# A second ring for compression and modulation weights, and their work spread over the attention groups, in a two-layer hybrid trunk

## What is computed

```python
for l in range(DEPTH):
    mod = c_act @ w_mod[l] + b_mod[l]
    shift, scale, gate = jnp.split(mod, 3, axis=-1)
    h = x * (1.0 + scale[:, None, :]) + shift[:, None, :]
    p = h @ w_in[l]
    ...
    # NSA: 2 key/value groups of 3 query heads; three branches per head
    kc = _rope(compress(k_cmp, pe_k, w1_k, w2_k), positions[:, cmp_end])
    vc = compress(v_cmp, pe_v, w1_v, w2_v)
    ...
    # gated delta rule, 6 heads; stick-breaking attention, 4 heads
    y = jnp.concatenate([y_nsa, y_gdn, y_sb], axis=-1) @ w_out[l]
    x = _layernorm(DEEPNORM_ALPHA * x + (1.0 + gate[:, None, :]) * y, ln_g[l], ln_b[l])

def compress(kv, pe, w1, w2):
    blk = kv[:, cidx] + pe[None, None, :, None, :]          # 31 blocks of 32 tokens
    flat = jnp.swapaxes(blk, 2, 3).reshape(b, n_cmp, NSA_KV_HEADS, CMP_LEN * HEAD_DIM)
    return jax.nn.silu(flat @ w1) @ w2
```

## Time and profile before

| | |
|---|---|
| median of three runs | 2878.05 us (2876.53 to 2882.39) |
| the profiled execution | 2874.73 us, its span 2872.9 us |
| mean granted clock of TensorE | 0.966 |
| busy: TensorE, VectorE, ScalarE, GpSimd | 89%, 46%, 23%, 45% |
| chain of work that ended last | TensorE 68%, VectorE 18%, issue 6%, ScalarE 4% |
| DMA | 314.81 MB, mean 110 GB/s |

### The profile page before, as it was taken

How to read it: one execution, slowest core, us unless ns; L and a number is a source line. 1 busy time by engine, 2 the same in 40 slices (tenths; PEclk the granted TensorE clock), 3 DMA queues, 4 the chain that set the end, 5 groups by cost and what they waited for, 6 DMA issues and landing times.

```text
span 2872.9 us, 40868 instructions
## 1 busy us (share of the span) xinstructions
PE 2543.4 (89%) x14320; PEld 2006.5 (70%) x14320; DVE 1312.7 (46%) x1915; ACT 648.5 (23%) x1168; POOL 1289.6 (45%) x1012
## 2 busy tenths in 40 slices
PE   0499889888999999998988999999899999997994
PEld 0387667666777777776866777777677777775773
DVE  8614651575555553464133143144555553457344
ACT  0301210112222222342003022012232222335000
POOL 7145334433444444445642634443344444543774
PEclk9999989999999999999999999999999999998997
DMA  9633444353221112444323311321111111344521
GB/s 357 230 118 105 140 148 130 120 162 102 62 64 60 60 60 92 143 164 154 96 80 130 102 59 59 125 67 52 60 60 59 60 60 62 129 141 145 205 88 73
DMA packets 82903, 314.81 MB, mean 110 GB/s; under 512 B 9974, under 2 KB 10230, under 8 KB 76950
## 3 DMA queue, kind: packets, MB, share of 16 engines
q1 hardware_dynamic: 76608, 295.51, 31.2%
q10 hardware_dynamic: 6108, 16.83, 1.6%
HBM read 303.92 MB, written 8.39 MB: 109 GB/s over the span
## 4 chain that ended last, share of the span: by engine, by line
PE 68%; DVE 18%; issue 6%; ACT 4%; POOLq 1%; DVEq 1%; ACTq 1%; POOL 1%; DMA 0%; SPq 0%
PE bank L450 14%; PE bank L452 13%; PE bank L451 13%; DVE arena L1243 10%; DVE acc L1243 5%; PE bank L831 4%; PE bank L832 4%; PE bank L833 4%; PE bank L430 2%; ACT arena L843 2%; DVE tiny L1243 2%; ACT L843 1%; PE bank L600 1%; PE bank L423 1%; PE bank L629 1%
## 5 line engine op out<-in xcount | busy, mean ns | idle before, releaser
L1194 POOL CAST w_hi<-ring 128x1024 fp32r<-128x1024 f32 (+1 forms) x328 | 345.7, 1054 | 1494.8 <-PE bank L452 964.0
L450 PE MATMUL bank<-h_hi,w_hi 128*128 128x512 f32 x2048 | 885.4, 432 | 39.0 <-POOLq L1200 35.6
L1198 POOL TENSOR_TENSOR w_lo<-ring,w_hi 128x512 fp32r<-128x512 f32 (+1 forms) x648 | 877.8, 1375 | 47.8 <-issue 0.9
L452 PE MATMUL bank<-h_hi,w_lo 128*128 128x512 f32 x2048 | 816.2, 399 | 0.9 <-issue 0.9
L451 PE MATMUL bank<-h_lo,w_hi 128*128 128x512 f32 x2048 | 815.3, 398 | 0.0
L450 PEld LDWEIGHTS bank<-h_hi,w_hi 128*128 128x128 f32 x2048 | 396.2, 193 | 144.3 <-POOLq L1200 36.0
L452 PEld LDWEIGHTS bank<-h_hi,w_lo 128*128 128x128 f32 x2048 | 393.4, 192 | 89.6
L451 PEld LDWEIGHTS bank<-h_lo,w_hi 128*128 128x128 f32 x2048 | 396.2, 193 | 81.7 <-issue 13.5
L843 ACT ACTIVATE arena<-bank 128x512 f32<-128x512 f32 (+6 forms) x352 | 166.3, 472 | 985.7 <-PE bank L452 395.0
L1243 DVE SCALAR_TENSOR_TENSOR acc<-ring,cact,acc 128x1024 f32<-128x1024 f32 x128 | 190.2, 1486 | 49.7 <-DMA ring<-in_stream 34.5
L831 PE MATMUL bank<-w_hi,h_hi 128*128 128x512 f32 x512 | 202.7, 396 | 7.2 <-POOLq L1200 7.2
(11 more groups left out here) (192 smaller groups left out, 2672.6 us busy)
## 6 DMA issues: line engine op xcount, KB each, us to landing
ring<-in_stream SPq DMA_DIRECT2D x480, 512.0 KB, 3.6
yT<-in_mod SPq DMA_DIRECT2D x32, 1024.0 KB, 6.3
arena<-in_x SPq DMA_DIRECT2D x1, 4096.0 KB, 15.9
arena<-in_x ACTq DMA_DIRECT2D x4, 1024.0 KB, 10.5
x_norm<-arena ACTq DMA_DIRECT2D x4, 1024.0 KB, 9.2
arena<-x_norm ACTq DMA_DIRECT2D x4, 1024.0 KB, 9.8
out<-arena SPq DMA_DIRECT2D x4, 1024.0 KB, 3.9
raw<-in_lns ACTq DMA_DIRECT2D x8, 256.0 KB, 5.8
```

The costliest lines, as they stand in the source:

```text
L450: mm(PJ[b][:, :], hi, h_hi[:, k, :], start=(k == 0), stop=False)
L452: last = mm(PJ[b][:, :], lo, h_hi[:, k, :], start=False, stop=(k == KT - 1))
L1194: pool.tensor_copy(w_hi[:, par, 0:w], ring[:, slot, 0:w])
L1198: pool.tensor_tensor(w_lo[:, par, at], ring[:, slot, at], w_hi[:, par, at].bitcast(F32), ALU.subtract)
```

## The change

- **A second ring.** `side`, four slots of 128x1024 in the upper half of `yT` (unused while the groups run), carries all D items and the M items of the groups. It has semaphores of its own, `side_in` and `side_free`. The main ring carries C items alone there. SyncE's loops are written out; after the load of half j it issues the side items of half j-3 (the last three together at the end of a group).
- **Compression in pieces and strips.** Piece d runs after half d of tiles 2 to 5, not in one block after tile 1. Its eight matmuls go in turn to four strips of 32 PSUM rows. ScalarE copies each set of four partial sums, and one matmul each with `sum4` adds them and transposes at once (it replaces L553). One tanh and one product on VectorE replace two each. Compressed keys are rotated last, after tile 7; the others a tile or two earlier than before.
- **Where the sums are.** Layer 0: one M item at halves 4 to 11, two at 12 to 19, one at 20 to 27. From half 16 on they stand behind the maximum of every other step. Layer 1: the gate's 32 M items leave the stick-breaking stage and go, 16 a group, to halves 8 to 23.
- **The mask matmul** uses plain float32 identity and mask (two records); the fp32r copies go.
- **Tables.** In `stick` ScalarE loads `natural_log_exp_and_others` right after the tanh. Its loop over the first two heads is written out.
- Some semaphores are merged (`pool_ready`, `act_ready`).

```diff
+def order_group(has_next):
+    mods, m = [], 0
+    for j in range(2 * GROUP_TILES):
+        n = (1 if 4 <= j < 12 or j >= 20 else 2 if j >= 12 else 0) if has_next else int(8 <= j < 24)
+        mods.append(list(range(m, m + n)))
+        m += n
+    return mods
...
+ORDER_SIDE = [[[("D", j - 4)] * (4 <= j < 12) + [("M", m) for m in mods[j]] for j in range(2 * GROUP_TILES)]
+              for mods in ORDER_MODS]
+ORDER_SB = [(SB_ITEMS, SB_2_ITEMS, SB_3_ITEMS)] * (DEPTH - 1) + [tuple(mixed(range(n), 0) for n in (LOT, 2, 1))]
...
+    blocks["sum4"] = (row % 32 == col[:, :N_CMP])
...
-        ident_r = sb("ident_r", [P, P], F32R)
-        causal_r = sb("causal_r", [P, P], F32R)
...
+        side = yT[:, 8:16, :].rearrange("p (a b) c -> p a (b c)", a=NS)
...
@@ sync
+                def load_side(g, item):
...
+                    slot, turn = side_place(l, g, item)
+                    sp.wait_ge(S(f"side_free{slot}"), turn + 1)
+                    sp.dma_start(side[:, slot, :], stream[STREAM[key]]).then_inc(S(f"side_in{slot}"), 16)
...
+                for g in range(KVH):
+                    for j, item in enumerate(ORDER_C):
+                        load(at["group"] + g * at["group_len"] + j, ("C", l, g, *item[1:]))
+                        if g == 0 and j == 7:
...
+                            if l == 0:
+                                sp.wait_ge(S("mod_used"), after("mod_used", 2 * KT))
+                            else:
+                                sp.wait_ge(S("y_split"), l * MIX_T)
+                        for ahead in ([j - 3] if j >= 3 else []) + ([25, 26, 27] if j == 27 else []):
+                            for what in ORDER_SIDE[l][ahead]:
+                                load_side(g, what)
...
@@ tensor
-                    def compress(which):
-                        pe.wait_ge(S("blocks_ready"), G * 2 + which + 1)
-                        for q4 in range(4):
...
-                            for i in range(CMP_LEN // 4):
...
-                                last = mm(TB[which][0:N_CMP, 0:HD], blocks_kv[which][:, t * N_CMP:(t + 1) * N_CMP],
-                                          ring[:, q4, i * HD:(i + 1) * HD],
-                                          start=(t == 0), stop=(t == CMP_LEN - 1))
+                    def compress(d):
...
+                        which, part = divmod(d, NS)
...
+                        for i in range(CMP_LEN // NS):
+                            t, strip = part * (CMP_LEN // NS) + i, i % NS * 32
+                            last = mm(TB[which][strip:strip + N_CMP, 0:HD],
+                                      blocks_kv[which][:, t * N_CMP:(t + 1) * N_CMP],
+                                      side[:, slot, i * HD:(i + 1) * HD],
+                                      start=(part == 0 and i < NS), stop=(part == NS - 1 and i >= CMP_LEN // NS - NS))
...
                     load_tile(0)
                     load_tile(1)
-                    compress(0)
-                    compress(1)
-                    load_tile(2)
...
+                    load_and_compress(2, 0)
+                    load_and_compress(3, 2)
+                    copied(2)
+                    rotate(0, kS)
+                    load_and_compress(4, 4)
...
+                        last = mm(hid_sum[:, which, :], cmp_part[:, which, :], C("sum4"), start=True, stop=True)
...
+                    load_tile(7, KT // 2, KT)
                     pe.wait_ge(S("cmp_copied"), G + 1)
...
+                    rotate(3, cmpb[:, 0, 0:N_CMP])
...
-                                mm(SB_[(u + 1) % 2][:, w - P:w], ident_r[:, :], causal_r[:, :],
+                                mm(SB_[(u + 1) % 2][:, w - P:w], ident, C("causal"),
...
@@ scalar
+                    def copy_parts(which):
...
+                        act.wait_ge(S(f"side_free{slot}"), after(f"side_free{slot}", turn + 1))
+                        fn(cmp_part[:, which, :], TB[which][:, 0:HD], ACT.Copy).then_inc(S("cmp_parts"), 1)
...
                         if s == (3 if last else 0):
                             fn(A(4), raw[:, 3, TAPS - 1:], ACT.Tanh, scale=0.5).then_inc(S("sb_ztanh"), 1)
+                            act.preload_act_table_set("natural_log_exp_and_others")
...
@@ vector
+                    add_mods(4)
+                    add_mods(5)
+                    rope(G * 6, kS[0:32, :], SEQ, slice(0, SEQ))
+                    for j in range(6, 10):
+                        add_mods(j)
+                    rope(G * 6 + 1, kW[0:32, :], SEQ, slice(0, SEQ))
...
+                    add_mods(12)
+                    rope(G * 6 + 2, qT[0][0:32, :], SEQ, slice(0, SEQ))
+                    add_mods(13)
                     first = CMP_LEN - 1
+                    rope(G * 6 + 3, cmpb[0:32, 0, 0:N_CMP], N_CMP, slice(first, first + (N_CMP - 1) * CMP_STRIDE + 1, CMP_STRIDE))
+                    add_mods(14)
+                    add_mods(15)
...
                         for s in range(NSA_STEPS):
-                            if s in MOD_STEPS[r]:
-                                add_mods(*MOD_STEPS[r][s])
...
                                 ts(tiny[:, u:u + 1], tiny[:, 30:31], -SCALE, None, M).then_inc(S("max_ready"), 1)
+                                if u % 2 == 0:
+                                    add_mods(16 + 4 * r + u // 2)
...
-                            for m in (2 * s, 2 * s + 1):
+                            for m in (2 * s, 2 * s + 1) if has_next else ():
                                 add_mod(m, items, l, kind, more, first_k)
```

More of the change, by code:

```diff
@@ L84, with stream_index, order_lots @@
 GROUP_TILES = 14
+def order_group(has_next):
[5 more added lines that the diff above has]
+    return mods
+ORDER_C = mixed(range(GROUP_TILES), 0)
+ORDER_MODS = [order_group(l < DEPTH - 1) for l in range(DEPTH)]
+ORDER_SIDE = [[[("D", j - 4)] * (4 <= j < 12) + [("M", m) for m in mods[j]] for j in range(2 * GROUP_TILES)]
+              for mods in ORDER_MODS]
+SIDE = [sum(side, []) for side in ORDER_SIDE]
+SIDE_AT = [KVH * sum(len(side) for side in SIDE[:l]) for l in range(DEPTH)]
+ORDER_SB = [(SB_ITEMS, SB_2_ITEMS, SB_3_ITEMS)] * (DEPTH - 1) + [tuple(mixed(range(n), 0) for n in (LOT, 2, 1))]
+def stream_index():
+    keys = []
+    for l in range(DEPTH):
+        for g in range(KVH):
+            for kind, *at in group_items(l < DEPTH - 1):
+                keys.append(("mod", l + 1, g, *at) if kind == "M" else (kind, l, g, *at))
+        lot, k = 0, 0
+        for items in [FIRST_TILE] + [GDN_ITEMS] * GDN_H + [SB_ITEMS] * (SB_H - 2) + [SB_2_ITEMS, SB_3_ITEMS]:
+            for kind, *at in items:
+                keys.append(("mod", l, 2, at[0] + 2 * k) if kind == "M" else ("lot", l, lot + at[0], at[1]))
+            lot += sum(item[0] == "C" for item in items) // 2
+            k += sum(item[0] == "M" for item in items) // 2
+        keys += [("out", l, n, k2) for n in range(TT) for k2 in range(KT // 2)]
+    return {key: i for i, key in enumerate(keys)}
+STREAM = stream_index()
+def order_lots(l):
+    keys, lot, k = [], 0, 0
+    sb, sb_2, sb_3 = ORDER_SB[l]
+    for items in [FIRST_TILE] + [GDN_ITEMS] * GDN_H + [sb] * (SB_H - 2) + [sb_2, sb_3]:
+        for kind, *at in items:
+            keys.append(("mod", l, 2, at[0] + 2 * k) if kind == "M" else ("lot", l, lot + at[0], at[1]))
+        lot += sum(item[0] == "C" for item in items) // 2
+        k += sum(item[0] == "M" for item in items) // 2
+    return keys
 LAYER_TILES = KVH * GROUP_TILES + (N_LOTS - 1) * LOT
@@ L87, with layout @@
 LEVELS = (2, 4, 8, 16, 32)
-def layout(has_next):
-    group = len(group_items(has_next))
+def layout(l):
+    group = len(ORDER_C)
+    sb, sb_2, sb_3 = ORDER_SB[l]
     at, n = {"group": SMALL_HALVES, "group_len": group}, SMALL_HALVES + KVH * group
@@ L106, in layout @@
     return at
-LAYOUTS = [layout(l < DEPTH - 1) for l in range(DEPTH)]
-STREAM_AT = [sum(a["end"] - SMALL_HALVES for a in LAYOUTS[:l]) for l in range(DEPTH)]
+LAYOUTS = [layout(l) for l in range(DEPTH)]
 HALVES_AT = [sum(a["end"] for a in LAYOUTS[:l]) for l in range(DEPTH)]
@@ L293, in build @@
             CREDITS[f"raw_free{i}"] = 1
+            CREDITS[f"side_free{i}"] = 1
         for i in range(LOT):
@@ L403, in _ @@
                     sp.dma_start(sm_all[:, :], small[l + 1]).then_inc(S("small_in"), 16)
-                load(at["out"], OUT_HALVES)
+                for n in range(TT):
+                    for k2 in range(KT // 2):
+                        load(at["out"] + n * (KT // 2) + k2, ("out", l, n, k2))
             for t in (1, 0, 2, 3):
                 if t == 0:
-                    sp.wait_ge(S("pool_out"), 1)
+                    sp.wait_ge(S("pool_ready"), 3)
                 else:
@@ L1108, in stick @@
                                 fn(h_hi[:, k, :], yT[:, k, :], ACT.Copy).then_inc(S("y_hi"), 1)
-                with act.Fori(0, SB_H - 2) as h:
+                for h in range(SB_H - 2):
                     stick(h, sb_fill)
@@ L1339, in _ @@
```

(3 more changed lines are left out.)

177 lines of the change are left out of this document (94 added, 83 removed).

## The result

The changed kernel takes **2782.2 us** (median of four runs, 2776.7 to 2783.2) against 2880.2 us (2876.5 to 2883.0) for the kernel before on the same chip. The ratio is 0.9656, 95% interval 0.9641 to 0.9670. Forecast were 2795 us, range 2757 to 2840. The profiled run took 2782.7 us, with a span of 2780.8.

What follows compares the result with a forecast made beforehand. TensorE was taken to set the pace of layer 1's heads, VectorE and the ring layer 0's. 2874.7 - 45 - 23 + 11 - 2 - 23 = 2792.7, with the median 3.3 above the profiled run: 2795 us, range 2757 to 2840.

Steps and rivals of the forecast that it cites:

- Compression: Groups' projection tiles: compression in blocks between halves, on four strips, without the wait for GpSimd, saves 45 us (bounds -52 and -10).
- The block: Eight compression matmuls between projection halves: 1.0 us each, between 0.8 with full strip overlap and 2.1 with none.
- The mask: Score steps of twelve heads: the exact mask matmul's second record adds 0.16 us, eight times a head, 15 us inside other terms.
- Heads, layer 0: Layer 0's heads in both groups: third -28.7, second -7, first +12.2 us, together -23 us.
- (b): Rival: sums in the groups cost what they cost now, 0.87 us each, as VectorE's time matters, not place; 2838 us, chance 0.10.
- The stall at the compressed softmax: Layer 0's first head: TensorE waits 5.0 us for VectorE's rotation, four sums, gate product and softmax, 11.6 us in all.
- Heads, layer 1: Layer 1's heads, with 16 new sums a group: first +2.0, second 1.3 + 0.8, third 1.3; both groups +11 us.
- Stick-breaking: Stick-breaking stage: layer 1 loses its 32 sums, and fewer table loads help the last heads; together -23 us.
- The rest: Clearing of the accumulator leaves the start of the delta stage, -1.8 us; out-projection, entry and the remaining delta stage unchanged.
- (a): Rival: the compression's column strips run one after the other, 32 x 1.1 us more; 2830 us, chance 0.16.
- (c): Rival: the new stalls stay away since VectorE runs ahead, and strips overlap fully; 2756 us, chance 0.16.
- (d): Rival: side loads waiting for VectorE block main loads in SyncE's one queue; slower, 2957 us at one half in three, chance 0.04.

Runs made afterwards that it cites:

- the pairs: The changed kernel with two compression blocks one behind the other after each whole projection tile, not one after each half: 2777.4 us.
- the preloads: The changed kernel without the two table preloads in a stick-breaking head, so ScalarE loads tables as the kernel before did: 2782.7 us.

## Why the prediction was nearly right, and where its terms were not

**Compression: forecast -45, measured -54 us** over the four stretches of tiles 1 to 7. The mechanism is shown. The block was the mis-sized term: 1.0 us taken, 0.77 measured, 8 blocks a group, 7 us in all. The lower bound, 0.8 for full overlap, was the value. Holding it back from full overlap had no row behind it; the only row near, two 64x64 tiles, overlapped fully. The other 2 us are in what the blocks displaced. The Trainium skill (TensorE: Matmul & The Clock Gate, Part 3) lets a weight load overlap only where the row groups differ, which would have made the block 2.1 us. The runs disagree: strips that share all rows overlap, 0.77 us. The trace of the kernel before disagreed already: at 303.82 us the weight load of L452 runs beside the matmul of L451, and both use all 128 rows.

**The mask: forecast +15 us, measured +12** over the heads. Nearly right in full: 0.13 us a matmul for 0.16.

**Heads, layer 0: forecast -23, measured -21.4.** Second heads 40.35 and 40.32 for 40.4, third 46.9 and 47.5 for 47.4, first 53.4 and 53.2 for 51.9. The numbers came out and the reason did not, which is luck: the hiding was put down to the place behind the maximum, and the run with the sums ahead of it is no slower. Right was that a lone sum costs little; wrong why, and even so 0.4 us against the 0.2 taken. (The recorded sum for the third head is 47.2 by its own terms, not 47.4, and its 0.6 has no row behind it.) The price of the kernel before (0.87, rival b) did not hold, though the premise of (b), that place doesn't matter, nearly did. The stall at the compressed softmax was named, and forecast at 5.0 us; it is 6.9. The timeline of the changed kernel, layer 0's first head, which begins at 246.00:

```profile
247.28 1.26 DVE L1345 TENSOR_TENSOR cmpb<-arena 32x31 f32<-32x31 f32 x1
248.72 6.83 DVE L1345 SCALAR_TENSOR_TENSOR acc<-yT,cact,acc 128x1024 f32<-128x1024 f32 x4 [0.17 <-issue]
254.61 3.73 POOL L1299 TENSOR_TENSOR w_lo<-ring,w_hi 128x512 fp32r<-128x512 f32 x2
255.73 1.49 DVE L1345 SCALAR_TENSOR_TENSOR arena<-arena 128x512 f32<-128x512 f32 x1 [0.18 <-issue]
...
260.65 1.06 PE L698 MATMUL bank<-cst,arena 128*31 128x128 f32 x4 [6.92 <-DVE arena L1345]
```

The rotation ends 2.5 us after the head's start, not 0.9, the sums take 7.0 for 6.6, the gate product 1.7 for 0.9, the softmax 3.4 for 3.2; that is 14.6 for 11.6 us, and TensorE asks at 7.7 instead of 6.7.

What the working left out is who runs beside VectorE. The gate product takes 1.49 us here, beside the second part of GpSimd's split (L1299), and 0.69 in layer 1's first head, where GpSimd stands idle at that moment. The same goes for the sums of 128x1024 in the changed kernel: all 60 that lie beside no L1299 take 1.28 or 1.29 us, the 68 beside one 1.28 to 2.39, 1.67 on average. The mean of 1.49 in the earlier trace rows mixes the two. That the one slows the other is read from these rows; no run tested it.

**Heads, layer 1: forecast +11, measured +15.7.** First heads are 4.8 and 4.0 us longer for 2.0, since the stall is 4.3 us and not 1.6. The chain was again sized too short: the two sums end 4.5 us after the rotation for 3.3, the softmax takes 4.6 for 3.2, both beside GpSimd's splits. Leaving the two late sums out takes 5.8 and 5.0 us away. Second 2.6 each for 2.1; third 0.7 and 1.0 for 1.3.

**Stick-breaking: forecast -23, measured -29.** Layer 1: 6.2 and 7.9 us in the full lots (13.3 forecast), 5.7 in the third (4.5), 3.5 in the last head (3.3). GpSimd waits for TensorE there and no longer for a DMA. Layer 0: 5.8 for 2. The step that gave its 2, shorter table loads in the last head, did not happen (39.0 us before, 39.4 after); the gain is in the two full lots (7.0 us), by the unrolled issue of loads, which the working passed over though the diff shows it. The tables are worth 4.6 us in layer 1, more than forecast and partly in the third lot.

**The rest** fell by 3 us for 2 (the clearing, and first tiles at either clock). Together the terms give 10 us more than forecast on the profiled run (2782.7 for 2792.7); 9 of it is compression, 6 stick-breaking and 1 the rest, less 6 in the heads. That the miss is 10 and not 16 is terms that err in opposite directions. The median misses by 13: the profiled run stands at it now and stood 3 us below it before. (By its terms the recorded sum would end at 2796, not 2795.)

**The rivals.** (a) serial strips: fell, 0.77 us against 2.06. (b) fell by its price. (c), full overlap without stalls: half true, the overlap came and the stalls too. (d) did not occur in the changed kernel as a loss: SyncE stood 12 us at side loads, but TensorE's waits for GpSimd were 0.5 us in layer 0's groups. Two experiments made its mechanism costly with one load more in a few halves, at one place a group, by some 4 to 8 us; that is far from the 14 such events that (d) needs, and says little about the chance of 0.04.

## What to carry to other kernels

Small matmuls that use few output rows go in strips side by side, also where they share the contraction rows; price them, as here, as records over strips plus a fixed 0.34 us each time the big matmuls are left, and put several together. Before work is moved onto an engine "that idles", list all its idle places in a step and what stands first in its queue after the move: most of the cost here came not from the score steps but from sums that stood ahead of one short softmax, and in two experiments from a shared ring whose next consumer stood waiting in its own queue. Size such a chain with the durations that its instructions have beside the other engines' work, not with a mean. A stretch that can be compared between two layers of one trace tells more than the total: two of the experiments (the pairs and the preloads) moved the total by less than 5 us, no more than chips and first tiles do.

## What the runs showed of the hardware that was not expected

- Four column strips with common rows overlap completely: 16 records of 128 columns add 0.43 us, on one strip 1.72 us.
- Going from 128x512 matmuls to such a block and back costs 0.33 to 0.34 us, with 16 records and with 32.
- Behind a pause of 14 to 15 us the second load came 0.86 to 0.88 us after the first when issued from a loop with an address from its counter, and 0.38 us when unrolled. The next two of the loop came 0.5 to 0.6 us apart, and unrolled the third came 1.1 us after the second, so that all four took 2.3 us either way.
- A VectorE product of 128x1024 with two operands in SBUF took 1.28 or 1.29 us in all 60 cases beside no L1299 of GpSimd, and 1.28 to 2.39 us in the 68 beside one.
- The same waits can cost 6 us more or not: layer 0's two groups, with some 4 us of new waits each, ran their first heads in 53.7 and 47.4 us at granted clocks of 0.87 and 1.00. What decides it stays open.
